# MLP down products: six of the eight sums of weight blocks in a chunk, made on VectorE or by adding transfers from GpSimd's queue

## The reference, cut to what matters

```
def sqrelu_mlp(h, w_up, w_down):               # h 512 x 1024
    return jnp.square(jax.nn.relu(h @ w_up)) @ w_down   # w_up 1024 x 4096, w_down 4096 x 1024

for i in range(2):
    h = rmsnorm(x, g_mix_pre[i]);  m = mixer_i(h)
    x = x + rmsnorm(m, g_mix_post[i])
    h = rmsnorm(x, g_ffn_pre[i])
    x = x + rmsnorm(sqrelu_mlp(h, mlp_w_up[i], mlp_w_down[i]), g_ffn_post[i])
```

## Time and profile before

| | before |
|---|---|
| time, median of 3 runs | 1161.71 us (1161.38 to 1161.81) |
| profiled execution, span from first to last instruction | 1160.8 us |
| TensorE busy | 1140.7 us, 98% of the span |
| VectorE busy | 901.5 us, 78% |
| ScalarE busy | 668.2 us, 58% |
| GpSimd busy | 201.5 us, 17% |
| mean granted TensorE clock | 0.996 |
| moved by DMA | 102.31 MB, 88 GB/s on average |

### The profile page before, as it was taken

The page is one execution under the profiler, slowest core; times in us unless marked ns, Lnnn a source line. Parts: engine busy times, 40 slices in busy tenths (PEclk is TensorE's granted clock), DMA queues, the critical chain, the costliest instruction groups (busy, mean ns, idle before and its releaser), DMA issues. The chain is left out here.

```text
span 1160.8 us, 16330 instructions
## 1 busy us (share of the span) xinstructions
PE 1140.7 (98%) x5662; PEld 961.7 (83%) x5662; DVE 901.5 (78%) x1385; ACT 668.2 (58%) x1152; POOL 201.5 (17%) x190
## 2 busy tenths in 40 slices
PE   8999999999999999999999999999999999999997
PEld 7788888888888888888888888888888888888886
DVE  5899965788479588589788888884788488586698
ACT  6778867565444353445786667665565453443453
POOL 5688860300000000002420010100300000000003
PEclk9999989999999999999999999999999999999999
DMA  5322123321522414312122322222423414215301
GB/s 170 98 66 72 37 75 109 110 73 45 173 73 85 170 37 150 105 37 57 53 55 60 86 72 54 73 74 73 146 73 116 135 40 154 100 37 182 109 19 73
DMA packets 103676, 102.31 MB, mean 88 GB/s; under 512 B 4621, under 2 KB 86541, under 8 KB 103610
## 3 DMA queue, kind: packets, MB, share of 16 engines
q1 hardware_dynamic: 103532, 101.29, 27.4%
q10 hardware_dynamic: 78, 0.16, 0.0%
HBM read 99.34 MB, written 2.10 MB: 87 GB/s over the span
## 5 line engine op out<-in xcount | busy, mean ns | idle before, releaser
L672 PE MATMUL psum<-hhi,whi 128*128 128x512 f32 x760 | 300.2, 395 | 0.8 <-DVE wlo L1792 0.5
L674 PE MATMUL psum<-hhi,wlo 128*128 128x512 f32 x760 | 296.3, 390 | 0.0
L673 PE MATMUL psum<-hlo,whi 128*128 128x512 f32 x760 | 296.0, 390 | 0.0
L1247 ACT ACTIVATE whi<-mraw 128x1024 fp32r<-128x1024 f32 x176 | 185.4, 1055 | 142.9 <-PE psum L969 113.6
L1803 DVE TENSOR_TENSOR wlo<-mraw,whi 128x1024 fp32r<-128x1024 f32 x176 | 214.4, 1224 | 42.3 <-ACT whi L1247 42.3
L967 PE MATMUL psum<-whi,aop_hi 128*128 128x512 f32 x448 | 174.9, 390 | 0.0
L969 PE MATMUL psum<-whi,aop_lo 128*128 128x512 f32 x448 | 174.4, 389 | 0.0
L968 PE MATMUL psum<-wlo,aop_hi 128*128 128x512 f32 x448 | 174.3, 389 | 0.0
L674 PEld LDWEIGHTS psum<-hhi,wlo 128*128 128x128 f32 x760 | 142.6, 188 | 30.5
L672 PEld LDWEIGHTS psum<-hhi,whi 128*128 128x128 f32 x760 | 142.8, 188 | 29.4 <-issue 1.8
L673 PEld LDWEIGHTS psum<-hlo,whi 128*128 128x128 f32 x760 | 142.9, 188 | 28.0
(11 more groups left out here) (266 smaller groups left out, 2003.3 us busy)
## 6 DMA issues: line engine op xcount, KB each, us to landing
mraw<-in_mlp_w_up SPq DMA_DIRECT2D x64, 512.0 KB, 5.1
mraw<-in_mlp_w_down SPq DMA_DIRECT2D x64, 512.0 KB, 4.5
wraw<-in_conv_pw_w SPq DMA_DIRECT2D x20, 512.0 KB, 4.5
wraw<-in_attn_w_in SPq DMA_DIRECT2D x16, 512.0 KB, 4.9
wraw<-in_attn_w_in SPq DMA_DIRECT2D x16, 256.0 KB, 3.1
wraw<-in_attn_w_o SPq DMA_DIRECT2D x8, 512.0 KB, 4.0
xin<-in_x SPq DMA_DIRECT2D x4, 512.0 KB, 6.8
wraw<-in_conv_pw_w SPq DMA_DIRECT2D x8, 256.0 KB, 6.7
```

The lines of the kernel that those rows point to most:

```text
L672: pe.matmul(o, whi[:, u, kb, :], xhi, start=start, stop=False)
L673: pe.matmul(o, whi[:, u, kb, :], xlo, start=False, stop=False)
L674: return pe.matmul(o, wlo[:, u, kb, :], xhi, start=False, stop=stop)
L1247: a.activation(split_unit(whi, e), raw_unit(c, e_), ACT.Copy).then_inc(s["m_hi"], 1)
```

## The change

VectorE keeps the two sums of P5. The other six of a chunk (P7, P6 and P4, two halves each) become transfers on GpSimd's queue that add: the source is the block in HBM, the destination the slot of `mraw`, with `accum_op=ALU.add`. `down_sums` stands in GpSimd's program between its work before and after each MLP, and issues them in the order P7, P7, P6, P6, P4, P4 for each chunk. ScalarE's `m_hi` waits for the landing of the transfer on one of six new semaphores. To make room for these, other semaphores are merged (`w0_loaded` into `m_raw`, `f_one` and `f_base` into `consts`, `stored` into `x_loaded0`), with the counts that are waited for moved along; this changes no instruction but its semaphore. The slots, the transfers on SyncE's queue and TensorE's program stay as they are.

```
+            def add_down(l, c, i, h):
+                gc, p = CHUNKS * l + c, raw_slots(c)
+                units = MLP_UNITS * l + UNITS * c + UP_UNITS
+                if i == P7:
+                    pool.wait_ge(m_raw[p[B12]], 32 * (2 * gc + 3))
+                    pool.wait_ge(s["t_sum"], 2 * gc + h + 1)
+                else:
+                    pool.wait_ge(s["m_ready"], units + 2 * {P6: P5, P4: P6}[i] + h + 1)
+                f, dh = PLUS_AT[PLUS[i]]
+                wd = mlp_w_down[l, c * D:(c + 1) * D, :].rearrange("(i f p) d -> f p i d", f=2, p=P)
+                to = mraw[:, p[BLOCK[i]], h * D:(h + 1) * D].rearrange("p (i d) -> p i d", d=D // 2)
+                g.dma_start(to, wd[f][:, 2 * h:2 * h + 2, dh * (D // 2):(dh + 1) * (D // 2)],
+                            accum_op=ALU.add).then_inc(sum_landed[i][h], 16)
+            def down_sums(l):
+                for c in range(CHUNKS):
+                    for i, h in ((P7, 0), (P7, 1), (P6, 0), (P6, 1), (P4, 0), (P4, 1)):
+                        add_down(l, c, i, h)
...
             add_squares(1)
+            down_sums(0)
...
             add_squares(3)
+            down_sums(1)
...
                 elif i in PLUS:
-                    act.wait_ge(s["t_sum"], 8 * g + SUM_NTH[i, e_ % 2])
+                    act.wait_ge(sum_landed[i][e_ % 2], 16 * (g + 1))
...
             def down_chunk(l, c):
                 g, n = CHUNKS * l + c, UNITS * c
-                add_block(g, P6, 0)
                 if c:
                     add_product(g, P1)
                 m_lo(l, n + 13)
-                add_block(g, P6, 1)
                 m_lo(l, n + 14)
-                add_block(g, P7, 0)
                 if c:
                     add_product(g, P2)
                 m_lo(l, n + 15)
-                add_block(g, P7, 1)
                 m_lo(l, n + 16)
                 m_lo(l, n + 17)
                 if c:
                     add_product(g, P5)
-                add_block(g, P4, 0)
                 m_lo(l, n + 18)
-                add_block(g, P4, 1)
```

More of the change, by code:

```diff
@@ L62 @@
 PLUS = {P5: B12, P7: B22, P6: B22, P4: B21}
-SUM_NTH = {(i, h): 2 * n + h + 1 for n, i in enumerate((P5, P6, P7, P4)) for h in range(2)}
+PLUS_AT = {B12: (0, 1), B22: (1, 1), B21: (1, 0)}
 PBANK = (0, 2, 0, 2, 4, 0, 6)
@@ L315, in build @@
     m_raw = tuple(s[f"mraw{r}"] for r in range(4))
+    sum_landed = {i: (s[n + "_sum0"], s[n + "_sum1"]) for i, n in ((P6, "v6"), (P7, "v7"), (P4, "v4"))}
     def flat(ap):
@@ L466, in _ @@
                 sp.wait_ge(s["tile_out"], n)
-                sp.dma_start(od[t], flat(xtok[:, t, :, :])).then_inc(s["stored"], 16)
-            sp.wait_ge(s["stored"], 16 * TB)
+                sp.dma_start(od[t], flat(xtok[:, t, :, :])).then_inc(s["x_loaded0"], 16)
+            sp.wait_ge(s["x_loaded0"], 16 * (TB + 1))
         @block.gpsimd
@@ L1241, in m_hi @@
                 if e_ < UP_UNITS:
-                    act.wait_ge(m_raw[p[e_ // 2]], 32 * (2 * g + 1))
+                    act.wait_ge(m_raw[p[e_ // 2]], 32 * (2 * g + 2))
+                elif i == P5:
+                    act.wait_ge(s["t_sum"], 2 * g + e_ % 2 + 1)
                 elif i in PLUS:
-                    act.wait_ge(s["t_sum"], 8 * g + SUM_NTH[i, e_ % 2])
+                    act.wait_ge(sum_landed[i][e_ % 2], 16 * (g + 1))
                 else:
-                    act.wait_ge(m_raw[p[BLOCK[i]]], 32 * (2 * g + 2))
+                    act.wait_ge(m_raw[p[BLOCK[i]]], 32 * (2 * g + 3))
                 a.activation(split_unit(whi, e), raw_unit(c, e_), ACT.Copy).then_inc(s["m_hi"], 1)
@@ L1337, in _ @@
             for c in range(STEPS):
-                act.wait_ge(s[f"w0_loaded{c}"], 32)
+                act.wait_ge(m_raw[c], 32)
                 for g in range(2):
@@ L2137, in s_lo, with add_block @@
                                 ALU.subtract).then_inc(s["s_ready"], 1)
-            def add_block(g, i, h):
+            def add_block(g, h):
                 l, c = divmod(g, CHUNKS)
                 p = raw_slots(c)
-                last_use = {P5: P1, P6: P5, P7: None, P4: P6}[i]
                 half = slice(h * D, (h + 1) * D)
[L2145 to L2152, removed]
+                dve.wait_ge(m_raw[p[B12]], 32 * (2 * g + 3))
+                dve.wait_ge(s["m_ready"], MLP_UNITS * l + UNITS * c + UP_UNITS + 2 * P1 + h + 1)
+                to = mraw[:, p[B11], half]
+                d.tensor_tensor(to, to, mraw[:, p[B12], half], ALU.add).then_inc(s["t_sum"], 1)
             def product_done(l, c, i, tt=1):
@@ L2186, in up_chunk @@
                             if c == 0:
-                                add_block(g, P5, 0)
-                            add_block(g, P5, 1)
+                                add_block(g, 0)
+                            add_block(g, 1)
                         relu(g, 2 * i + 1)
@@ L2418, in _ @@
             dve.wait_ge(s["f_hi"], 1)
-            dve.wait_ge(s["f_base"], 2)
+            dve.wait_ge(s["consts"], 9)
             dve.wait_ge(s["sel_part"], 9)
```

25 lines of the change are left out of this document (10 added, 15 removed).

## The result

The changed kernel takes 1175.14 us in the median of its four executions, the kernel before 1161.70 us. One of the four took 4045.58 us, with the clock at full level, and none of the later ones was like it; the median of the other three is 1173.49 us (1171.77 to 1176.79), and the ratio is formed without it: 1.0104 with a 95% interval of 1.0085 to 1.0124. So the change makes the kernel 1% slower. The profiled execution is the fastest one, 1171.77 us, its span 1170.04 us. Against the profiled execution of before (1160.78) that is 9.26 us more.

A forecast was written before the change was run, and what follows sets the result against it. TensorE's fixed pace was taken to bound the kernel inside the down parts. 8.4 + 4.6 = 13.0 us lost less 1.0 gained gave +12.0: 1172.8 profiled, 1173.7 us; range 1159.6 to 1196.

The forecast's parts named there:

- The relief: VectorE in the chunks: 48 sums of 1.22 us removed, 58.6 us of busy time, counting nothing there.
- the 1.0 us of gain: After layer 0's last chunk and at the program's end: 1.0 us gained together, between 0 and 3.65.
- Behind layer 0: After layer 0's last chunk, VectorE no longer late: 0.7 us gained, between 0 and 3.0.
- at the end: VectorE's last sum after TensorE's last MLP matmul: 0.3 us gained, at most 0.65.
- The transfer: One adding transfer, wait's clearing to landing: 4.5 landing + 1.3 adding + 1.3 issue = 7.1 us, between 3.5 and 14.4.
- the second read: In an adding transfer, reading the slot as well as the block: 1.3 us for another 0.52 MB, bounds 0 and 1.3.
- Chunks 1 to 3: Six chunks, TensorE ahead of unit 14: transfer 7.1 less 5.7 to spare, 1.4 us late each, 8.4 lost.
- the allowance of 5.7: Chunks 1 to 3, P6's first half: 5.7 us to spare for landing before TensorE wants unit 14.
- Chunk 0: Two chunks, P2's copy behind P6's second landing: 7.1 less 4.8 to spare, 2.3 us late each, 4.6 lost.
- rival C: Adding transfers slow in themselves, P6's two queueing behind each other and behind P7's: 1213 us at 12 us each; chance 0.12.
- Rival B: P6's sums land in time, under about 5.5 us, leaving only the 1.0 us gain: 1160.7 us; chance 0.30.
- Rival A: The forecast itself: TensorE late by 0.6 to 3.7 us a chunk, 1164 to 1192 us; chance 0.50.

The follow-up runs named there:

- the second profile: The changed kernel run again unaltered, against more runs of the kernel before: 1175.74 us, ratio 1.01; its profiled execution took 1175.79 us.
- with the 48 waits: The changed kernel with 48 more waits at the head of TensorE's program, which shift its instruction fetches: 1173.69 us, ratio 1.0097 against the kernel before.
- P6 alone: The changed kernel with only P6's sums as adding transfers, P7's and P4's on VectorE: 1183.65 us, ratio 1.0188 against the kernel before.

## Why the prediction was right

The forecast was 1173.7 us, slower, and 1175.14 was measured (1173.49 without the execution of 4045.58 us). Its mechanism is the one found: only P6, only ahead of unit 14, longest in chunk 0. Its time is near for a worse reason: the terms of the sum were off and made up for each other, which is luck. Point by point:

- **The relief is worth nothing inside the chunks.** Shown by leaving the sums out: 0.9999. Of the 1.0 us of gain at the two other places, 0.60 showed in the profile. Behind layer 0 I took 0.7 and nothing came: TensorE's waits there are 1.8 and 1.2 us as before. (The stretch is 0.10 us shorter, but it is between 320.2 and 322.3 us long over the profiles.) All of it is at the end, where I took 0.3: L2274's 1.73 us are 1.23 after, and VectorE's last sum, which started 0.65 us behind the end of the last matmul, now starts 0.03 behind it (1162.86), after waiting for it:

```profile
1162.89 0.69 DVE L2295 TENSOR_TENSOR acc<-acc,psum 128x512 f32<-128x512 f32 x1 [1.02 <-PE psum L994]
```

- **The transfer.** I took 7.1 us from the wait's clearing to the landing. It was 6.0 to 6.4 for P6's first half (7.1 in the last chunk). The parts were off in both directions: a plain transfer from GpSimd lands in 4.0, not 4.5; moving the data takes 1.4 more, near the 1.3 that I took for the second read; but of the 1.3 for the issue only 0.5 comes on top of the 4.0, and 0.3 passes between the wait's clearing and the issue. (The 10.7 us of the earlier trace rows that bounded it from above is an up block's; the slowest of the down blocks took 9.6.)
- **Chunks 1 to 3.** 6 x 1.4 = 8.4 us predicted, 3.8 measured (0.28 to 0.65 in five, 1.41 in the last). This term was mis-sized, because of the 7.1: the allowance of 5.7 was right. The last chunk's share is the instruction packet, which I had no idea of.
- **Chunk 0.** 2.3 us each predicted; the gaps were 2.58 and 2.69. This came out right partly by luck: the second half landed 7.5 us after its `m_lo`, not 7.1, because it queued behind the first (2.5 us between landings at about 200 GB/s, half the plain rate of the earlier trace rows). I had put that queueing into rival C, with a far higher price.
- **The clock.** It was nowhere in the sum. Layer 0's chunk 0 lost 4.35 us, 1.8 more than its gap; where both chunks 0 have the half clock, as in the second profile, it is 3.5 us (8.7 lost, 5.2 of it gaps). It filled the place of what chunks 1 to 3 did not lose.
- **Rival B**, that the sums land in time, was what two rules of the Trainium skill would give. DMA: Bandwidth & Descriptors (Anatomy of one DMA, the SWDGE path) has 3.2 us for 0.52 MB, an estimate by that page; the plain transfers of GpSimd took 4.0, 0.8 more. Collectives: The Full Stack (The bandwidth ceiling) has a second source read and no cycles for the add. The trace agrees with a doubled cost on the DMA engines (13.2% for 6.5%, at equal bytes) and a second read would account for the 1.4 us more for moving the data, but GpSimd's instruction also becomes 0.49 us longer, which the page doesn't say. By both the landing would be 4.4, and it was 5.9: the chain had 5.7 and 4.8 to spare, so this decided the sign.
- **Slips in the working.** Rival A's 1164 us goes with transfers of 5.9 us, which are 0.2 and 1.1 us late, not 0.6; lateness of 0.6 in chunks 1 to 3 gives 1167. The upper bound of 1196 adds 35.2 to the span of 1160.8 and not to the time, which would give 1197. Neither bears on the forecast.

So the total was near because two errors cancelled. In the first profile (9.26 us more in all) chunks 1 to 3 lost 4.6 us less than forecast and chunk 0 2.6 more; 1.06 us are the shorter start. In the second (13.3 us more) it is 4.1 less and 4.1 more, nearly all by the clock and by the second half's queueing, neither of which was in the sum. The 1.5 us between forecast and median lie within the spread of the executions (1171.77 to 1176.79).

## What to carry to other kernels

Work taken off an engine is worth nothing in a stretch where nothing waits for that engine. Ask what slack the new path's latency has to fit into, and give the path to the sums that have the slack: here P7's and P4's 32 transfers were free and P6's 16 cost 1%. If a transfer must be late, move ahead of it what doesn't need it, above all what frees a bank: moving two instructions took 1.0% down to 0.1%. An idle gap of TensorE can cost more than its own length, through the clock behind it (here 2.58 us cost 4.35 in one chunk, and 2.69 us cost 2.87 in another, where the clock stayed up). No version here beats the kernel before; the best ones equal it (1.000 and 1.0001).

## What was not expected of the hardware

- An adding transfer of 512 KB makes 272 packets (256 of 2 KB with data) where a writing one makes 144 (128 of 4 KB), and two of them land 2.5 us apart, at about 200 GB/s. GpSimd is held 1.22 us by each for 0.73, and the landing is 5.9 us for 4.0: 0.5 us of that before the first data packet, 1.4 behind it.
- Beside the adding transfers SyncE's loads of the up blocks land later, 6.0 us in the median for 5.1 before; with P6's back on VectorE it is 5.2. TensorE waited for none of them here.
- TensorE's granted clock fell to 0.50 for 3.4 us behind gaps of 2.56 to 3.01 us in 7 of 9 cases (changed kernel 1 of 2, run again 2 of 2, with the 48 waits 1 of 2, P6 alone 3 of 3), and behind none of the 1.7 us or less. The length of the gap does not decide it: behind 2.69 and 2.76 us the clock stayed full, behind 2.56 it fell. Why is open.
- A 16 KB instruction packet 1.8 to 3.5 us behind the issue of P6's adding transfer puts its landing off by some 1 us (8 of 8 cases); moved to 0.7 us, before the transfer's first data, it costs nothing. That it holds one of the DMA engines is my reading; the runs show only the time. The writing transfers were not delayed by such a packet (3.2 and 3.5 us behind the issue, landings of 4.1 and 4.0), so what makes the adding ones open to it is not shown.
